# A second sparse lookup: 64 of 256 tokens taken out of the dense pass of layer 1, the dense products cut from 256 to 192 columns

## The reference

```python
def peer(h, w_q, sub_keys, u, v):            # 8 heads, 128 keys per side, 16 picks a head
    q = (h @ w_q).reshape(T, PEER_HEADS, 2, PEER_QDIM // 2)
    s = jnp.einsum('thpd,hpnd->thpn', q, sub_keys)
    sv, si = lax.top_k(s, PEER_TOPK)
    cand = (sv[:, :, 0, :, None] + sv[:, :, 1, None, :])...
    fv, fi = lax.top_k(cand, PEER_TOPK)
    idx = (i1 * PEER_NKEYS + i2)             # 128 picks of 16384 experts for each token
    g = softmax(fv)
    act = gelu(einsum('td,ted->te', h, u[idx]))
    out = einsum('te,ted->td', g * act, v[idx])
```

## Time and profile before

| | us |
|---|---|
| median of three runs | 4296.46 (4284.73 to 4301.57) |
| the profiled execution, its own time | 4287.59 |
| its span in the trace | 4285.8 |
| PE busy in the span | 4187.1 |
| DVE / ACT / POOL busy | 3071.4 / 1793.0 / 1331.9 |
| TensorE's mean granted clock | 0.993 of 2.4 GHz |

### The profile page before, as it was taken

How to read it: one execution, slowest core, us unless ns; L and a number is a source line. 1 busy time by engine, 2 the same in 40 slices (tenths; PEclk the granted TensorE clock), 3 DMA queues, 4 the chain that set the end, 5 groups by cost and what they waited for, 6 DMA issues and landing times.

```text
span 4285.8 us, 61414 instructions
## 1 busy us (share of the span) xinstructions
PE 4187.1 (98%) x24279; PEld 3729.0 (87%) x24279; DVE 3071.4 (72%) x4936; ACT 1793.0 (42%) x2976; POOL 1331.9 (31%) x699
## 2 busy tenths in 40 slices
PE   7999999999999999999999999999999999999999
PEld 5888778888888799867999999999999799998887
DVE  5775558877887686465599798788887675554776
ACT  3233352233233544263234786333334645444444
POOL 0000200000000100000378666777772058444443
PEclk9999999999999999999999999999999999999999
DMA  7543215544555364212477899999994166678884
GB/s 276 221 165 146 84 43 203 223 179 191 220 194 203 109 253 184 79 40 77 142 243 250 301 342 343 367 359 353 358 352 166 60 199 220 226 245 285 288 287 168
DMA packets 287199, 926.35 MB, mean 216 GB/s; under 512 B 19648, under 2 KB 171328, under 8 KB 212800
## 3 DMA queue, kind: packets, MB, share of 16 engines
q1 hardware_dynamic: 250048, 788.18, 51.8%
q0 software_dynamic: 36864, 134.23, 8.7%
HBM read 837.40 MB, written 84.93 MB: 215 GB/s over the span
## 4 chain that ended last, share of the span: by engine, by line
PE 86%; DVE 5%; DMA 4%; ACT 2%; POOL 1%; issue 1%; SPq 0%; ACTq 0%; POOLq 0%; DVEq 0%
PE bank L1132 25%; PE bank L1133 24%; PE bank L1134 24%; PE bank L1570 3%; DMA gates<-work 1%; PE bank L1325 1%; PE bank L1127 1%; PE bank L1122 1%; PE bank L1118 1%; PE bank L1337 1%; POOL weight_ring_low L2906 1%; PE bank L1362 1%; DVE work L2635 1%; DVE weight_ring_low L2246 1%; DMA work<-in_up_rows,work 1%
## 5 line engine op out<-in xcount | busy, mean ns | idle before, releaser
L2906 POOL TENSOR_TENSOR weight_ring_low<-weight_ring,up_high 128x1024 fp32r<-128x1024 f32 x233 | 586.4, 2521 | 1069.7 <-ACT up_high L1994 1067.6
L1134 PE MATMUL bank<-peer_h_high,weight_ring_low 128*128 128x256 f32 (+2 forms) x2240 | 698.3, 312 | 0.0
L1132 PE MATMUL bank<-peer_h_high,up_high 128*128 128x384 f32 (+1 forms) x2048 | 643.4, 314 | 14.3 <-POOL weight_ring_low L2906 7.4
L1133 PE MATMUL bank<-h_low,up_high 128*128 128x384 f32 (+1 forms) x2048 | 633.8, 309 | 0.0
L2081 ACT ACTIVATE down_high<-weight_ring 128x1024 fp32r<-128x1024 f32 x256 | 257.1, 1052 | 523.5 <-PE bank L1134 518.0
L1134 PE MATMUL bank<-h_high,weight_ring_low 128*128 128x512 f32 (+1 forms) x1280 | 463.9, 362 | 0.0
L1132 PE MATMUL bank<-h_high,in_high 128*128 128x512 f32 (+1 forms) x1216 | 441.1, 363 | 0.3
L1133 PE MATMUL bank<-h_low,in_high 128*128 128x512 f32 (+1 forms) x1216 | 440.8, 362 | 0.0
L2870 POOL TENSOR_SCALAR h<-work,params 128x256 f32<-128x256 f32 x12 | 11.8, 997 | 1376.7 <-PE bank L1477 874.6
L2662 DVE TENSOR_TENSOR weight_ring_low<-weight_ring,down_high 128x1024 fp32r<-128x1024 f32 x128 | 314.8, 2459 | 160.8 <-ACT down_high L2081 160.8
L1134 PEld LDWEIGHTS bank<-peer_h_high,weight_ring_low 128*128 128x128 f32 x2240 | 426.4, 190 | 3.7
(11 more groups left out here) (417 smaller groups left out, 10074.5 us busy)
## 6 DMA issues: line engine op xcount, KB each, us to landing
weight_ring<-in_up SPq DMA_DIRECT2D x128, 1024.0 KB, 6.0
weight_ring<-in_down SPq DMA_DIRECT2D x128, 1024.0 KB, 5.6
weight_ring<-in_mod_w SPq DMA_DIRECT2D x112, 1024.0 KB, 4.8
weight_ring<-in_ffn_in SPq DMA_DIRECT2D x88, 1024.0 KB, 6.9
weight_ring<-in_ffn_out SPq DMA_DIRECT2D x64, 704.0 KB, 5.7
gates<-work SPq DMA_DIRECT2D x40, 1024.0 KB
gelu<-work SPq DMA_DIRECT2D x64, 384.0 KB
work<-gates SPq DMA_DIRECT2D x32, 768.0 KB, 12.8
```

The costliest lines, as they stand in the source:

```text
L1132: mm(dst, w_high, a_high, start=first, stop=False)
L1133: mm(dst, w_high, a_low, start=False, stop=False)
L1134: return mm(dst, w_low, a_high, start=False, stop=last)
L2906: G.tensor_tensor(ring_low[:, slot, w], ring[:, slot, w], up_high[:, n % 3, :].bitcast(F32), ALU.subtract)\
```

## The change

Layer 1 now treats its last 64 latents as layer 0 treats a tile: they leave the dense pass, which has 192 tokens instead of 256, and their picks are gathered. Since 64 tokens would fill half the partitions, two picks of a token stand side by side: partition p < 64 has pick k of token 192+p, partition 64+p has pick k+64 of the same token. So there are 64 gathers of u and 64 of v, 512 KB each.

```diff
-ORDER = {0: (3, 2, 0, 1), 1: (0, 1)}
-PICKED = 3
-DENSE = {0: 3 * P, 1: TL}
-SLOT_PICKS = PH * TOPK
+ORDER = {0: (3, 2, 0, 1), 1: (1, 0)}
+PACK = {0: 1, 1: 2}
+PICKED = {l: P // n for l, n in PACK.items()}
+TOKENS = {0: T, 1: TL}
+DENSE = {l: TOKENS[l] - PICKED[l] for l in PACK}
+ROUTED = {0: 3, 1: 2}
+SLOT_PICKS = {l: PH * TOPK // n for l, n in PACK.items()}
+TILE_PLACES = {0: {...},
+               1: {1: (6, 8, 9, 11, 12, 13, 14, 15)}}
@@ routing_units: units beside a tile, beside a block
-    tile, between, blocks = (16, 2, DENSE[0] // BLOCK) if l == 0 else (28, 4, DENSE[1] // BLOCK)
+    tile, between, blocks = (16, 2, DENSE[0] // BLOCK) if l == 0 else (24, 4, DENSE[1] // BLOCK)
@@ products beside a half block; splits that DVE takes
+def half_rows(l, q):
+    return 1 + q % 2 if l == 0 else 2
@@ split_beside
-    return [units[-1] for units in gates] if l == 1 else list(rest[1:-2:2])
+    return list(rest[1:-2:2])
@@ PE: h of the picked tokens is turned to rows, twice over
+                            for g in range(PACK[l]):
+                                dst = ps[KEY_BANK + 2 * k + kc // 4][n * g:n * g + n, kc % 4 * P:kc % 4 * P + P]
...
+                                    i = mm(dst, src, ident, start=True, stop=True)
@@ PE: the picks of the 64 tokens move to both halves of the partitions
+                def move_tables():
+                    n = PICKED[l]
+                    pe.wait_ge(tables_made, 1)
+                    pe.wait_ge(routed_copied, r0 + 1)
+                    for k, table in enumerate((pick_at_f, pick_gates)):
+                        for g in range(PACK[l]):
+                            i = mm(ps[TURN_BANK][n * g:n * g + n, k * n:k * n + n], ident[:, P - n:P], table[:, n * g:n * g + n], start=True, stop=True)
+                    i.then_inc(tables_moved, 1)
...
-                        if l == 0 and j == 0 and i == 2:
+                        if j == 0 and i == 2:
                             turn_h()
+                        if l == 1 and j == 1 and i == 2:
+                            move_tables()
@@ PE, down half: rows_product, turn_back_rows and their copies go; layer 1 takes chunk_product
-                    if l == 1:
-                        for half in range(2):
-                            o = rows_product(n, half)
-                        if k:
-                            o.then_inc(panel_done, 1)
-                        return
...
+                            mm(ps[dc][:, picked_tokens], picked_sum[:, dc, :], pick_at_f[:, 0:PICKED[l]], start=True, stop=True)\
+                                .then_inc(picked_turned, 1)
@@ DVE: takes the tables over before it routes the second tile
+                def read_tables():
+                    n = PICKED[l]
+                    dve.wait_ge(tables_moved, 1)
+                    V.tensor_copy(pick_index[:, 0:n], ps[TURN_BANK][:, 0:n]).then_inc(index_ready, 1)
+                    V.tensor_copy(pick_gates[:, 0:n], ps[TURN_BANK][:, n:2 * n]).then_inc(tables_read, 1)
...
+                    if l == 1 and j == 1:
+                        read_tables()
                     dve.wait_ge(keys_scored, 4 * (t0 + j + 1))
@@ DVE, gates of layer 1: no third multiplication (ACT does it, weigh_marks), no split; two picked products a half block
-                    dve.wait_ge(marks_ready, 2 * g0 + q + 1)
-                    V.tensor_tensor(first, first, spread(routed[:, 2, tokens], 2, P), ALU.mult).then_inc(marks_weighted, 1)
...
-                    if l == 1 and q % 2 == 0:
-                        split_up(split_beside(l)[q // 2])
-                    if l == 0:
-                        for c in range(1 + q % 2):
-                            picked_product(picked_at["half", q, c])
+                    for c in range(half_rows(l, q)):
+                        picked_product(picked_at["half", q, c])
@@ POOL: gathers in layer 1 too
-                    for q in range(SLOT_PICKS):
-                        if l == 0 and gathered_behind(q) == n:
+                    for q in range(SLOT_PICKS[l]):
+                        if gathered_behind(l, q) == n:
                             gather(q)
```

325 lines of the change are left out of this document (140 added, 185 removed).

## The result

The changed kernel takes 4362.92 us (median of four runs, 4355.92 to 4368.76), the kernel before 4299.01 in the same rounds: a ratio of 1.0155, with a 95% interval of 1.0138 to 1.0172. It is slower by 1.55%, twice what I forecast (0.8%, 4330 us), inside the range. The profiled execution has a span of 4367.0 us.

A forecast was written before the change was run, and what follows sets the result against it. The prediction took PE's products to bound the kernel. PE's own up-half work -25.5, second tile +28, gates +28, down half +6 gave +36.5 us: 4324 on the profiled 4287.6, 4333 as median, forecast 4330, range 4285 to 4380.

The forecast's parts named there:

- All fit: Down half: DVE 5.2, POOL 2.4 plus one gather, DMA 5.3 us fit PE's 5.52 us a pair; 2 us added for collisions.
- Products of 192 columns: PE's layer 1 up and down products: 115 ns each, set by loading the stationary matrix, between bounds of 93 and 120.
- The rivals with 93 ns: Columns alone set PE's product time: suppliers hold, about 4307 us, chance 0.15; or down half follows, 4244 us, chance 0.12.
- the one that ended faster: Columns alone at 93 ns, and the down half follows, 286 us instead of 348: 4244 us, chance 0.12.
- the dear product of 120 ns: Rival: a 192-column product costs as much as one of 256, 120 ns, adding 27 us: 4357 us, chance 0.20.
- the first rival: Product as dear as with 256 columns: some 5400 products 5 ns dearer, +27, 4357 us, chance 0.20.
- The second tile: Layer 1's up half: PE waits 8 us at first, then for late gathers; +25 for waits, +3 for clock, +28 us.
- the late places 13 to 15: Second tile: last three picked products, done by about 72 us; their gathers make POOL wait for DVE, up to 9 us each.
- +3 for the clock: Second tile: 3 us added for PE's products at a low clock after waits, within the +28 us.
- The gates: Up half, 12 blocks: 17.0 us each, 2.4 above PE's 14.6, from gathers waiting for products and tight transfers: +28 us.
- The down half: Layer 1: products at 115 ns add 4 us for 128 units, collisions 2 us: +6 us.
- The rest and the end: Up half's remaining units cost nothing, up to +8; the program's end costs 0, between -2 and +2 us.

The follow-up runs named there:

- gates_dve: Changed kernel, but from the gates' second half block on DVE, not POOL, makes the low parts of all units there: 4320.36 us, ratio 1.0056 to the kernel before.
- down_dve: Changed kernel, but in layer 1's down half DVE makes both low parts of a pair and POOL only gathers: 4345.25 us, ratio 1.0116 to the kernel before.
- pool_busy: Best version (4274.81 us, edits of several runs together) plus one useless POOL subtraction for each pair of layer 1's down half: 4309.00 us, ratio 1.0039.
- gates_lag: Changed kernel with the gates' gathers one unit later in POOL's order: 4362.73 us, ratio 1.0160 to the kernel before.
- up_columns: Kernel before with 192, 128, then 64 moving columns in layer 1's up products, the other tokens' products left out: 4509.8 us in one run.
- tile_places: Changed kernel with later gather places beside the second tile, 28 units a tile instead of 24, first four gathers behind four units: 4351.58 us, ratio 1.0133.

## Why the prediction was right in direction and short in size

The step that failed is the one that lets DVE's products and POOL's subtractions run side by side, "All fit" with 2 us for collisions in the down half, waits only at handovers in the gates. They take turns: in the down half a pair takes 5.64 us where PE needs 5.38, in the gates a product of 1.22 us takes 5.42. A second term was mis-sized, the clock beside the second tile.

**Products of 192 columns** at 115 ns, set by the load: right, 112 measured. The rivals with 93 ns fall, and with them the one that ended faster; so does the dear product of 120 ns. The sentence by which 107 ns would take some 20 us off does not fit the 5400 products that the first rival counts: 8 ns on each are 43 us, unless the suppliers hold.

**The second tile**, +28 us: 37 measured (103.6 less 24 units of 2.69 and some 2 us for tables and picks; the forecast's own units were 2.76). The first wait came as worked out, 7.6 us at the 28th unit, and the sum is near, 23.3 us where 25 were forecast. That is in part luck: of the rest, 5.8 us stand at the 36th unit, where I had none, since DVE did place 8 only 32 us after it had the tables and POOL came for it before; the late places 13 to 15 cost 9.6 us instead of 17. Mis-sized is "+3 for the clock": the products behind the waits cost 14 us.

**The gates**, 17.0 us a block: 18.0 measured, 216 us for twelve instead of 204; without waits they take 171 (gates_dve). POOL's own time came as worked out (14.3 us for 14.6), and so did one wait of 2.0 us at a handover. What the working lacked is the second wait, 1.9 us a block: it let DVE's products run beside POOL's subtractions, and there they are held. gates_dve, with the same gathers, products and transfers, takes all of the excess away, but with POOL's own work as well; so the size of the hold's share rests on the timelines. The 16.3 us of transfers a block were too many as well: the share of 0.98 of 14.3 us is 14.0.

**The down half**, +6 us: 22.3 measured. This is the same step at its plainest: 5.2 us of DVE, 2.4 and one gather of POOL, 5.3 of transfers, and "All fit", with 2 us for collisions in all. They would fit side by side; DVE's work and POOL's subtraction go one after the other, and 5.65 us is more than 5.38. That makes some 17 us, and the wait at the start the rest. down_dve and pool_busy show it from both sides. My 5.2 was itself part hold: free of POOL, DVE needs 3.4 us a pair with one low part, 4.55 with both. The trace before has the hold in 62 of 63 pairs; DVE's low part, 1.14 us alone, beside POOL's:

```profile
4102.41 2.58 DVE L2662 TENSOR_TENSOR weight_ring_low<-weight_ring,down_high 128x1024 fp32r<-128x1024 f32 x1 [1.57 <-ACT down_high L2081]
```

```profile
4101.51 2.41 POOL L2915 TENSOR_TENSOR weight_ring_low<-weight_ring,down_high 128x1024 fp32r<-128x1024 f32 x1 [3.09 <-ACT down_high L2081]
```

**The rest and the end** at 0: right as a sum. The rest is 93.5 us for 32 units, 86 of PE's own and 1.7 for the last half block, which is counted here; what is left is mostly a wait of 2.1 us and products at the lower clock level (granted 0.96 in the stretch). Before, PE waited 3.3 us for DVE between the last up and the first down product instead. From the last product of the down half to the end it is 15.5 us, 15.3 before.

Put together: the up half +48.1 instead of +30.5, the down half +22.3 instead of +6. Against the forecast the down half is 16 us dearer, the gates 12 and the second tile 9; the cheaper products give some 3 back, which leaves the missing 34. The 16 are the shared turn for the most part, as two runs show. That the 12 are too is read from timelines, and the 9 are the clock's.

The rows for it were there. The earlier trace rows show a product of 1.22 us that took 2.63 where it met POOL's subtraction; I priced it as an accident of single instructions, and did not ask what share of DVE's time POOL's subtractions cover: four of 2.4 us in a block of 14.6.

The Trainium skill states it ("SBUF — State Buffer", section "SBUF: two separate sides"): VectorE and GpSimd share a port pair under an exclusive lock, which holds against a VectorE instruction with two SBUF inputs while GpSimd reads SBUF; whoever starts first has it for the whole instruction. The trace agrees (the product at 3778.00 was held for 4.3 us, 5.42 in all; the marks beside it, with one input in PSUM, were not), and shows one thing more: the waiting product did not get its turn between two subtractions that followed each other, nor between three in gates_lag.

## What to carry to other kernels

When an operation moves to an engine that has "room", add up DVE's and POOL's work with two inputs in SBUF in one column, not two, and leave out what reads PSUM: a POOL subtraction of 2.4 us replaced by a DVE one of 1.2 made this kernel faster although DVE was the busier engine. Ask of each gather that reuses a buffer who delays the product it waits for; where it is the gathering engine itself, no later place in the queue helps. Fewer moving columns do not make a product cheaper once the load of the stationary matrix is the longer part (0.112 us here, at 192 and at 64), and may cost the clock.

## What the runs showed of the hardware that I had not expected

- The granted clock fell to 0.50 (1.2 GHz) with PE busy 150.0 of 150 us, when it multiplied 64 columns with a stationary 128x128 each; with 192 columns it was 1.00 in the first tile after and in the gates of gates_dve, and 0.96 in the first tile of up_columns, with waits of 1.2 to 2.0 us.
- Over a stretch with four waits of 4 to 8 us it was 0.80 at 192 columns and 0.87 at 256 with nearly the same waits.
- A subtraction 128x1024 with two SBUF inputs takes 1.14 us on DVE and 2.4 on POOL. While POOL's runs, DVE's does not (held 4.3 us at 3778.00, and 7.96 us in all over three in gates_lag).
- It works in the other direction too: POOL's subtraction at 3592.49 took 3.05 us, with a DVE product running until 3593.22, and one in tile_places took 4.4, with `keyed` running for its first 2.2. The issue of an indirect gather takes 0.93 to 0.95 us beside marks (37 in the changed kernel) and up to 2.25 beside a DVE instruction with both inputs in SBUF; it then ends some 0.8 us after that one.
